# A tuned transformer kernel on one core: the seven-product scheme for gate and up of four feed-forward stages

## The chip, the core and the metric

The kernel runs on one core of a Trainium2 chip. The metric is the device time of one execution in microseconds (us), the median of several runs. The core's engines run side by side, each with its own queue that is worked off in order, and they wait for each other by semaphores: TensorE (PE in the rows; PEld is its loading of weights), VectorE (DVE), ScalarE (ACT), GpSimd (POOL) and SyncE (SP), which here issues the loads of weights.

## The reference, cut to what matters

Two transformer blocks follow each other on 512 tokens of width 1024. The first has two layers, each with a feed-forward part, a mixer and another feed-forward part; the second has 16 more tokens in front, and again a feed-forward part, a mixer and a feed-forward part. That makes six feed-forward stages with an inner width of 2816:

```python
def swiglu_ffn(x, w_gu, w_down):
    a, u = jnp.split(x @ w_gu, 2, axis=-1)
    return (jax.nn.silu(a) * u) @ w_down

def first_block(x, w_in, w_out, ...):
    for l in range(DEPTH):
        x = layer_norm(DEEPNORM_ALPHA * x + 0.5 * swiglu_ffn(x, ffn1_w_gu[l], ffn1_w_down[l]), ...)
        x = layer_norm(DEEPNORM_ALPHA * x + hybrid_mixer(x, ...), ...)
        x = layer_norm(DEEPNORM_ALPHA * x + 0.5 * swiglu_ffn(x, ffn2_w_gu[l], ffn2_w_down[l]), ...)
    return x
```

The change concerns the four feed-forward stages of the first block, and in them the products with `w_gu` (gate and up).

## The kernel before

**Layout.** Activations are kept with features on the partitions: `x` is 8 tiles (k) of 128 features by 512 tokens. A matmul multiplies a weight tile of 128x128 with 512 columns of one such tile. Every product is formed in three parts for precision: a number is split into a high part, rounded to the matmul's format, and a low part, the rest. The three are high weight by high x, low weight by high x, and high weight by low x. `pe_piece` (L387) does that: for each k three matmuls at L397, L400 and L403, all added up in one bank of PSUM.

**Weights.** They come in pieces of 128x1024 (8 tiles of 128x128, 512 KB). SP loads piece u into `w_raw[u % 4]` (`sp_load`), ACT casts it to `w_hi` (`act_split`, L340), and DVE subtracts to get `w_lo` (`dve_split`, L351). There are four slots of `w_hi`/`w_lo` in a ring; a cast waits until the piece that had its slot has been used by TensorE. A load waits for the low part of the piece that had its `w_raw`. In mixers GpSimd makes some of the low parts (L366).

**A feed-forward stage** (`ffn`, L480). There are 22 pairs of pieces: gate tile f and up tile f. TensorE does piece after piece (48 matmuls of 512 columns for a pair). ACT then makes silu of the gate product out of PSUM (L574), DVE multiplies it by the up product (L596), ACT casts the result to `h_hi` (L578), and DVE makes `h_lo` (L606). Then 8 tiles of the down product follow, each in three pieces, and the norm (`FfnNorm`, `MixNorm`). The order on each engine is written out by hand: the loops `ffn_pe`, `ffn_act` and `ffn_dve` run over steps s, one for each piece, with splits three pieces ahead. The first 3 or 5 pieces of three of these stages are done as a group, since x comes out of the norm tile by tile; the very first stage has no group.

**Elsewhere.** `Prepare` puts a small table of the second block (a product of 383 columns, some short operations, a store) into the first stage. The two feed-forward stages of the second block, the mixers and the norms go by the same lines and aren't touched, apart from slots.

## Time and profile before

| what | value |
|---|---|
| median of 3 runs | 3092.79 us (3091.29 to 3094.11) |
| span of the profiled execution | 3090.1 us |
| TensorE busy | 3043.6 us, 98% of the span |
| weight loads (PEld) busy | 2548.2 us, 82% |
| VectorE busy | 1421.9 us, 46% |
| ScalarE busy | 1158.2 us, 37% |
| GpSimd busy | 379.7 us, 12% |

The runs are about 2.7 us longer than the span that the profile covers, from the first to the last instruction of the program. The duration of a matmul in a row is that of one in a pipeline, so neighbours overlap: what it costs is read from the distance of the starts.

### The profile page before, as it was taken

What the parts mean: (1) busy time and instruction counts of PE and PEld (TensorE: products, weight loads), DVE (VectorE), ACT (ScalarE), POOL (GpSimd) and SP (SyncE); (2) the same over time, 40 slices, a digit from 0 to 9 for tenths busy, and PEclk for the clock granted to TensorE, in tenths of its full rate; (3) what the DMA queues carried; (4) which work ended last, traced back from release to release, by engine and by line L of the source; (5) the groups of instructions that cost most, each with busy time, mean ns of one, the idle gap of its engine ahead of it and who ended that gap; (6) DMA issues with size and microseconds to landing.
All of it is one profiled execution on the core that took longest, in us unless ns stands there. A gap on an engine that the chain in (4) does not pass through costs nothing.

```text
span 3090.1 us, 39392 instructions
## 1 busy us (share of the span) xinstructions
PE 3043.6 (98%) x16494; PEld 2548.2 (82%) x16494; DVE 1421.9 (46%) x2120; ACT 1158.2 (37%) x1868; POOL 379.7 (12%) x319
## 2 busy tenths in 40 slices
PE   9999999999999999999999999899999999999999
PEld 7888877888888888887788888899999767788888
DVE  4333465653335333356583333744423766554432
ACT  3322376442223322146553221522223456543221
POOL 0000143300001000014320000200002323200000
PEclk9999999999999999999999999999999999999999
DMA  4223331132332322332123223222233211122232
GB/s 161 96 94 89 93 103 62 55 110 96 94 93 66 117 95 92 94 118 67 55 76 103 95 90 95 75 96 89 86 89 102 80 38 35 41 95 93 93 93 77
DMA packets 76496, 269.62 MB, mean 87 GB/s; under 512 B 8720, under 2 KB 9008, under 8 KB 76064
## 3 DMA queue, kind: packets, MB, share of 16 engines
q1 hardware_dynamic: 74448, 260.08, 26.3%
q0 software_dynamic: 1872, 7.04, 0.7%
q8 instruction: 130, 2.13, 0.3%
q14 instruction: 46, 0.38, 0.0%
HBM read 264.97 MB, written 2.11 MB: 86 GB/s over the span
## 4 chain that ended last, share of the span: by engine, by line
PE 90%; DVE 7%; ACT 2%; issue 1%; DMA 0%; SPq 0%; POOL 0%; DVEq 0%; ACTq 0%
PE psum L397 25%; PE psum L400 25%; PE psum L403 25%; PE psum L461 3%; PE psum L473 2%; PE psum L416 1%; PE psum L420 1%; PE psum L418 1%; PE psum L696 1%; PE psum L2840 1%; DVE z_sum L853 1%; DVE x L865 1%; DVE x L858 1%; DVE b_rank L3115 0%; PE psum L1881 0%
## 5 line engine op out<-in xcount | busy, mean ns | idle before, releaser
L351 DVE TENSOR_TENSOR w_lo<-w_raw,w_hi 128x1024 fp32r<-128x1024 f32 (+1 forms) x444 | 554.7, 1251 | 1260.5 <-ACT w_hi L340 1260.4
L397 PE MATMUL psum<-x_hi,w_hi 128*128 128x512 f32 (+1 forms) x2800 | 964.0, 368 | 1.1 <-ACT neg_mean L2911 0.8
L400 PE MATMUL psum<-x_hi,w_lo 128*128 128x512 f32 (+1 forms) x2800 | 949.8, 363 | 0.9 <-DVE w_lo L351 0.9
L403 PE MATMUL psum<-x_lo,w_hi 128*128 128x512 f32 (+1 forms) x2800 | 945.2, 362 | 0.1
L340 ACT CAST w_hi<-w_raw 128x1024 fp32r<-128x1024 f32 (+1 forms) x490 | 503.7, 1029 | 1172.7 <-PE psum L403 1137.1
L397 PEld LDWEIGHTS psum<-x_hi,w_hi 128*128 128x128 f32 x2800 | 500.0, 188 | 109.0 <-issue 18.6
L400 PEld LDWEIGHTS psum<-x_hi,w_lo 128*128 128x128 f32 x2800 | 499.6, 188 | 88.0 <-issue 4.8
L403 PEld LDWEIGHTS psum<-x_lo,w_hi 128*128 128x128 f32 x2800 | 500.4, 189 | 84.7 <-DVE x_lo L3349 0.4
L397 PE MATMUL psum<-h_hi_ffn,w_hi 128*128 128x512 f32 (+1 forms) x792 | 296.9, 375 | 0.0
L400 PE MATMUL psum<-h_hi_ffn,w_lo 128*128 128x512 f32 (+1 forms) x792 | 292.2, 369 | 0.0
L403 PE MATMUL psum<-h_lo_ffn,w_hi 128*128 128x512 f32 (+1 forms) x792 | 290.7, 367 | 0.0
L397 PEld LDWEIGHTS psum<-h_hi_ffn,w_hi 128*128 128x128 f32 x792 | 149.0, 188 | 28.6 <-issue 1.0
L403 PEld LDWEIGHTS psum<-h_lo_ffn,w_hi 128*128 128x128 f32 x792 | 148.8, 188 | 28.2
L400 PEld LDWEIGHTS psum<-h_hi_ffn,w_lo 128*128 128x128 f32 x792 | 148.6, 188 | 27.2 <-issue 1.0
L366 POOL TENSOR_TENSOR w_lo<-w_raw,w_hi 128x512 fp32r<-128x512 f32 x92 | 119.7, 1324 | 248.6 <-ACT w_hi L340 248.5
L397 PE MATMUL psum<-h_hi_b_ffn,w_hi 128*128 128x264 f32 (+2 forms) x550 | 148.6, 316 | 0.0
L400 PE MATMUL psum<-h_hi_b_ffn,w_lo 128*128 128x264 f32 (+2 forms) x550 | 148.1, 315 | 0.0
L403 PE MATMUL psum<-h_lo_b_ffn,w_hi 128*128 128x264 f32 (+2 forms) x550 | 147.7, 314 | 0.0
L1031 POOL TENSOR_TENSOR z_sum<-x 128x512 f32<-128x512 f32 x4 | 5.2, 1299 | 1054.7 <-DVE x L1003 1054.7
L578 ACT CAST h_hi_ffn<-hid 128x512 fp32r<-128x512 f32 x88 | 54.6, 621 | 163.8 <-DVE hid L596 163.8
L403 PEld LDWEIGHTS psum<-h_lo_b_ffn,w_hi 128*128 128x128 f32 x550 | 93.2, 188 | 7.1
L397 PEld LDWEIGHTS psum<-h_hi_b_ffn,w_hi 128*128 128x128 f32 x550 | 93.1, 188 | 7.0
(386 smaller groups left out, 3388.3 us busy)
## 6 DMA issues: line engine op xcount, KB each, us to landing
w_raw<-in_ffn_gu SPq DMA_DIRECT2D x176, 512.0 KB, 3.3
w_raw<-in_ffn_down SPq DMA_DIRECT2D x64, 512.0 KB, 3.5
w_raw<-in_w_in SPq DMA_DIRECT2D x44, 512.0 KB, 3.3
w_raw<-in_b_gate SPq DMA_DIRECT2D x44, 512.0 KB, 3.3
w_raw<-in_b_up SPq DMA_DIRECT2D x44, 512.0 KB, 3.3
w_raw<-in_b_down SPq DMA_DIRECT2D x32, 512.0 KB, 3.5
w_raw<-in_ffn_down SPq DMA_DIRECT2D x32, 384.0 KB, 3.1
w_raw<-in_b_in SPq DMA_DIRECT2D x24, 512.0 KB, 3.3
```

Source lines behind the costliest of these rows:

```text
L340: nc.scalar.copy(w_hi[s][:, 0:n], w_raw[r][:, 0:n]).then_inc(*w_high.inc(u))
L351: nc.vector.tensor_tensor(w_lo[s][:, 0:n], w_raw[r][:, 0:n], w_hi[s][:, 0:n].bitcast(F32), ALU.subtract).then_inc(*w_low_dve.inc(u))
L366: nc.gpsimd.tensor_tensor(w_lo[s][:, c], w_raw[r][:, c], w_hi[s][:, c].bitcast(F32), ALU.subtract).then_inc(*w_low_pool.inc((u, half)))
L397: nc.tensor.matmul(out, w_h, hi[:, c], start=first and i == 0, stop=False)
L400: nc.tensor.matmul(out, w_l, hi[:, c], start=False, stop=False)
L403: done = nc.tensor.matmul(out, w_h, lo[:, c], start=False, stop=final and i == n - 1)
L416: nc.tensor.matmul(out, w_h, hi[:, c], start=j == 0, stop=False)
L418: nc.tensor.matmul(out, w_l, hi[:, c], start=False, stop=False)
L420: done = nc.tensor.matmul(out, w_h, lo[:, c], start=False, stop=j == KT // 2 - 1)
L461: nc.tensor.matmul(out, w_h, x_part[:, c], start=first, stop=False, skip_group_check=True)
L473: done = nc.tensor.matmul(out, w_l, x_hi[:, k, c], start=False, stop=k == KT - 1, skip_group_check=True)
L578: nc.scalar.copy(h_hi[:, f - 1, cols], hid[(f - 1) % 2][:, cols]).then_inc(*h_high.inc(f - 1))
```

## The change

In the stages `ffn1_0`, `ffn2_0`, `ffn1_1` and `ffn2_1` the pairs f = 0 to 3 stay as they were. Pairs 4 to 21 go through a new class `Combined`. It takes gate and up together as a 2 by 2 product of blocks: the two halves of the contraction (4 tiles of k each) and the two halves of the tokens (a and b, 256 columns each). With G1, G2 and U1, U2 for the two halves of a gate and an up piece, and X1a, X1b, X2a, X2b for the quarters of x, eight block products become seven:

| product | weights | x | bank |
|---|---|---|---|
| m1 | G1 | X1a | P |
| m2 | G2 | X2a | Q |
| m3 | s4 = s2 + G2 | X2b | R |
| m4 | U2 | t4 = -n2 - X2a | P |
| m5 | s1 = U1 + U2 | n1 = X1a - X1b | R |
| m6 | s2 = s1 + G1 | n2 = -n1 - X2b | P |
| m7 | s3 = U1 + G1 | t3 = X2b - X1b | P |

Gate a is m1 + m2; gate b is m1 + m6 + m5 + m3; up b is the negative of m1 + m6 + m7 + m5; up a is the negative of m1 + m6 + m7 + m4. Each product is 4 k by 3 parts, 12 matmuls of 256 columns.

What is new besides the products:

- x side, once a stage, in steps s = 1 to 5 of the direct part: `dve_turned`, `act_turned`, `dve_turned_low` make n1, n2, t3, t4 with high and low parts, 16 operations of DVE and 8 of ACT on 512 columns. t3 and t4 are put where `x` lies (`x_turned`); after the last m4 GpSimd rebuilds x as `x_hi + x_lo` (`pool`, 8 operations), and the norm waits for that (`rebuilt`).
- weight side, for each pair: DVE makes the sums s1, s2, s4 (into `sq_sum`, `square`) and s3 (into `w_raw` in place). The splits are of five blocks instead of two pieces: s1 and s3 (512 columns each, one slot), gate (1024), up's second half (512), and s2 with s4 as one ("later", 1024).
- results, for each pair: ACT copies three intermediate results out of PSUM (`act_copy`: r after m5, p1 after m1, p2 after m6). DVE joins gate a, gate b and up b, and makes h in two halves (`dve_first_half`, `dve_second_half`). silu now reads SBUF. The cast and the low part of h stay.
- `slot_plan` gives the four slots fixed roles in these pairs (sums, gate, up, later). `w_raw` of a gate piece is given back after s3, that of an up piece after the low part of its second half.
- the first down piece is done between m7 and m4 of the last pair (`fill`).
- `h_hi` and `h_lo` have 512 columns instead of 528, the tables of `Prepare` get their own places, `Prepare` moves to other steps, and GpSimd's scratch memory for DMAs is set to 4096.

```diff
+COMBINED = {"ffn1_0": 4, "ffn2_0": 4, "ffn1_1": 4, "ffn2_1": 4}
+HALF_K = KT // 2
+WIDTH = SEQ // 2
+            def pe_product(self, name, f):
...
+                for k in range(HALF_K):
...
+                    pe.wait_ge(*self.high.at((block, f)))
+                    nc.tensor.matmul(self.out(b), w_h, hi, start=opens and k == 0, stop=False,
+                                     skip_group_check=True)
+                    pe.wait_ge(*self.low.at((block, f)))
+                    nc.tensor.matmul(self.out(b), w_l, hi, start=False, stop=False,
+                                     skip_group_check=True)
+                    done = nc.tensor.matmul(self.out(b), w_h, lo, start=False,
+                                            stop=k == HALF_K - 1, skip_group_check=True)
+            def pe(self, fill):
...
+                for f in range(first, FT + 1):
+                    if f <= last:
+                        pe.wait_ge(*(self.joined.at(("gate_b", f - 2)) if f >= first + 2
+                                     else self.direct_left(self.r_bank(f))))
+                        self.pe_product("m5", f)
+                    if f > first:
+                        pe.wait_ge(*self.copied.at(("p2", f - 1)))
+                        self.pe_product("m7", f - 1)
+                    if f <= last:
...
+                        self.pe_product("m1", f)
+                        pe.wait_ge(*(self.joined.at(("gate_a", f - 1)) if f > first
+                                     else self.direct_left(self.q_bank)))
+                        self.pe_product("m2", f)
+                    else:
+                        fill()
+                    if f > first:
+                        pe.wait_ge(*self.joined.at(("up_b", f - 1)))
+                        self.pe_product("m4", f - 1)
+                    if f <= last:
+                        pe.wait_ge(*self.copied.at(("p1", f)))
+                        self.pe_product("m6", f)
+                        pe.wait_ge(*self.copied.at(("r", f)))
+                        self.pe_product("m3", f)
...
+            def act_high(self, name, f):
...
+                elif name == "later":
+                    act.wait_ge(*self.summed.at(("s4", f)))
...
+                if f > self.f0:
+                    act.wait_ge(*self.product_made.at((used_by, f - 1)))
...
+            def act_hidden(self, f):
+                act.wait_ge(*self.first_half.at(f))
+                act.wait_ge(*self.second_half.at(f))
+                nc.scalar.copy(self.h_hi[:, f, :], self.h[f % 2][:, TOK]).then_inc(
...
+            def pool(self):
+                pool.wait_ge(*self.product_made.at(("m4", FT - 1)))
...
-    nc = bacc.Bacc("TRN2", target_bir_lowering=False, num_devices=1)
+    nc = bacc.Bacc("TRN2", target_bir_lowering=False, num_devices=1,
+                   dynamic_dma_scratch_size=4096)
```

**The order on TensorE**, at the start of the first combined pair of the first stage. A row is one matmul with its columns; `t_hi` and `t_lo` are n1 and n2 of the x side. Before, in the middle of a piece:

```order
L397 MATMUL psum<-x_hi,w_hi0 128x512
L400 MATMUL psum<-x_hi,w_lo0 128x512
L403 MATMUL psum<-x_lo,w_hi0 128x512
L397 MATMUL psum<-x_hi,w_hi0 128x512
L400 MATMUL psum<-x_hi,w_lo0 128x512
```

After, where m5 ends and m1 begins:

```order
L677 MATMUL psum<-t_hi_ffn1_0,w_hi0 128x256
L680 MATMUL psum<-t_hi_ffn1_0,w_lo0 128x256
L682 MATMUL psum<-t_lo_ffn1_0,w_hi0 128x256
L677 MATMUL psum<-x_hi,w_hi1 128x256
L680 MATMUL psum<-x_hi,w_lo1 128x256
L682 MATMUL psum<-x_lo,w_hi1 128x256
```

A pair is now 84 matmuls of 256 columns in products of 12, where it was 48 of 512.

**The order on VectorE** in the middle of gate and up. Before, one pair and the start of the next:

```order
L596 TENSOR_TENSOR hid1<-hid1,psum 128x512
L351 TENSOR_TENSOR w_lo0<-w_raw0,w_hi0 128x1024
L606 TENSOR_TENSOR h_lo_ffn1_0<-hid1,h_hi_ffn1_0 128x512
L351 TENSOR_TENSOR w_lo1<-w_raw1,w_hi1 128x1024
L596 TENSOR_TENSOR hid0<-hid0,psum 128x512
```

After, twelve of the fifteen operations of a step: gate b, later low, s3, up b, s3 low, s1, s2, s4, gate a, s1 low, gate low, first half. The second half (L875, 256 columns), up low (L811, 512) and h low (L881, 512) follow.

```order
L849 TENSOR_TENSOR hid0<-psum,z_sum 128x256
L811 TENSOR_TENSOR w_lo3<-square,w_hi3 128x1024
L832 TENSOR_TENSOR w_raw3<-w_raw3,w_raw2 128x512
L857 SCALAR_TENSOR_TENSOR up_b_ffn1_0<-psum,neg_mean 128x256
L811 TENSOR_TENSOR w_lo0<-w_raw3,w_hi0 128x512
L832 TENSOR_TENSOR sq_sum<-w_raw1 128x512
L832 TENSOR_TENSOR square<-sq_sum,w_raw0 128x512
L832 TENSOR_TENSOR square<-square,w_raw0 128x512
L844 TENSOR_TENSOR hid1<-psum,z_sum 128x256
L811 TENSOR_TENSOR w_lo0<-sq_sum,w_hi0 128x512
L811 TENSOR_TENSOR w_lo1<-w_raw0,w_hi1 128x1024
L866 SCALAR_TENSOR_TENSOR hid0<-psum,hid0 128x256
```

A pair is four operations before and fifteen after.

**The order on ScalarE** at the same place. Before:

```order
L574 ACTIVATE hid1<-psum 128x512
L340 CAST w_hi3<-w_raw3 128x1024
L578 CAST h_hi_ffn1_0<-hid1 128x512
L340 CAST w_hi0<-w_raw0 128x1024
L574 ACTIVATE hid0<-psum 128x512
```

After, one whole step: up high, h high, copy p2, later high, silu, copy r, s3 high, copy p1, s1 high, gate high.

```order
L749 CAST w_hi2<-w_raw1 128x512
L772 CAST h_hi_ffn1_0<-hid1 128x512
L766 COPY z_sum<-psum 128x256
L749 CAST w_hi3<-square 128x1024
L788 ACTIVATE hid0<-hid0 128x512
L766 COPY neg_mean<-psum 128x256
L749 CAST w_hi0<-w_raw3 128x512
L766 COPY z_sum<-psum 128x256
L749 CAST w_hi0<-sq_sum 128x512
L749 CAST w_hi1<-w_raw0 128x1024
```

A pair is four operations before and ten after; the later cast now stands behind the h cast and a copy.

## Rows read from the trace of the kernel before

**Rows 1.** The page: engines, clock in 40 slices, chain that ended last, loads.

```profile
PE 3043.6 (98%) x16494; PEld 2548.2 (82%) x16494; DVE 1421.9 (46%) x2120; ACT 1158.2 (37%) x1868; POOL 379.7 (12%) x319
...
PEclk9999999999999999999999999999999999999999
...
PE 90%; DVE 7%; ACT 2%; issue 1%; DMA 0%; SPq 0%; POOL 0%; DVEq 0%; ACTq 0%
...
w_raw<-in_ffn_gu SPq DMA_DIRECT2D x176, 512.0 KB, 3.3
```

**Rows 2.** Timeline, VectorE, first stage: start us, duration us, operation, [idle before].

```profile
31.99 1.23 DVE L351 TENSOR_TENSOR w_lo<-w_raw,w_hi 128x1024 fp32r<-128x1024 f32 x1 [3.73 <-ACT w_hi L340]
...
43.11 1.23 DVE L351 TENSOR_TENSOR w_lo<-w_raw,w_hi 128x1024 fp32r<-128x1024 f32 x1 [3.73 <-ACT w_hi L340]
```

**Rows 3.** Timeline, TensorE, last down tile of the first stage, 45 matmuls apart.

```profile
373.80 0.28 PE L403 MATMUL psum<-h_lo_ffn,w_hi 128*128 128x256 f32 x1
...
379.09 0.28 PE L403 MATMUL psum<-h_lo_ffn,w_hi 128*128 128x256 f32 x1
```

**Rows 4.** Timeline, TensorE, output product in runs of 12; a run begins at 603.75.

```profile
603.64 0.28 PE L420 MATMUL psum<-x_lo,w_hi 128*128 128x256 f32 x1
603.75 0.28 PE L416 MATMUL psum<-x_hi,w_hi 128*128 128x256 f32 x1
603.87 0.28 PE L418 MATMUL psum<-x_hi,w_lo 128*128 128x256 f32 x1
```

**Rows 5.** Groups by shape, 130 to 250 us: count, busy us, mean ns, idle.

```profile
L397 PEld LDWEIGHTS psum<-x_hi,w_hi 128*128 128x128 f32 x173 | 32.5, 188 | 7.8
...
L351 DVE TENSOR_TENSOR w_lo<-w_raw,w_hi 128x1024 fp32r<-128x1024 f32 x21 | 25.7, 1225 | 78.4 <-ACT w_hi L340 78.4
L340 ACT CAST w_hi<-w_raw 128x1024 fp32r<-128x1024 f32 x21 | 22.1, 1052 | 64.1 <-PE psum L403 64.1
...
L606 DVE TENSOR_TENSOR h_lo_ffn<-hid,h_hi_ffn 128x512 fp32r<-128x512 f32 x10 | 6.8, 685 | 0.0
L578 ACT CAST h_hi_ffn<-hid 128x512 fp32r<-128x512 f32 x11 | 6.8, 621 | 20.8 <-DVE hid L596 20.8
```

**Rows 6.** Groups by shape, whole span: other shapes of VectorE and ScalarE.

```profile
L858 DVE SCALAR_TENSOR_TENSOR x<-psum,x 128x256 f32<-128x256 f32 x96 | 36.9, 419 | 0.2
...
L1022 DVE TENSOR_TENSOR x<-x,neg_mean 128x512 f32<-128x512 f32 x24 | 14.8, 688 | 0.0
```

**Rows 7.** The same view, ScalarE.

```profile
L568 ACT ACTIVATE hid<-hid 128x512 f32<-128x512 f32 x22 | 13.9, 633 | 52.7 <-DVE hid L616 52.7
...
L2014 ACT CAST y_hi<-psum 128x256 fp32r<-128x256 f32 x16 | 5.9, 368 | 11.3 <-PE psum L1881 11.3
```

**Rows 8.** Timeline around 105 us: hand-overs and overlaps.

```profile
104.65 1.05 ACT L340 CAST w_hi<-w_raw 128x1024 fp32r<-128x1024 f32 x1 [1.73 <-PE psum L403]
...
105.60 0.59 ACT L574 ACTIVATE hid<-psum 128x512 f32<-128x512 f32 x1
105.73 1.22 DVE L351 TENSOR_TENSOR w_lo<-w_raw,w_hi 128x1024 fp32r<-128x1024 f32 x1 [3.46 <-ACT w_hi L340]
...
106.88 0.68 DVE L606 TENSOR_TENSOR h_lo_ffn<-hid,h_hi_ffn 128x512 fp32r<-128x512 f32 x1
```

**Rows 9.** Timeline, VectorE: an operation that needs the one before it.

```profile
2000.10 0.70 DVE L596 TENSOR_TENSOR hid<-hid,psum 128x528 f32<-128x528 f32 x1
2000.83 0.71 DVE L601 TENSOR_TENSOR hid<-hid,z_sum 128x528 f32<-128x528 f32 x1
```

**Rows 10.** Timeline around 2708 us: last matmul of a product, and its reader.

```profile
2707.78 0.28 PE L420 MATMUL psum<-x_lo,w_hi 128*128 128x256 f32 x1
...
2708.10 0.42 DVE L2338 TENSOR_TENSOR x<-x,psum 128x256 f32<-128x256 f32 x1 [1.00 <-PE psum L420]
```

**Rows 11.** The chain of waits at the program's start: start us, us, what.

```profile
5.20 6.52 DMA w_raw<-in_ffn_gu
```

**Rows 12.** Timeline, GpSimd, start of the second block's mixer.

```profile
2369.55 4.23 POOL L3223 DMA_DIRECT2D b_q_lat<-bias_rows  x8
...
2381.62 3.96 POOL L366 TENSOR_TENSOR w_lo<-w_raw,w_hi 128x512 fp32r<-128x512 f32 x2 [6.26 <-ACT w_hi L340]
```

More of the change, by code:

```diff
@@ L205, in widened, with combined_pieces @@
     return [n for n in first if n.startswith("mix_") or n in ("ffn2_0", "ffn2_1", "ffn1_1")]
+def combined_pieces(first):
+    return {first[name] + i: name for name, f0 in COMBINED.items()
+            for i in range(2 * f0, 2 * FT)}
 def slot_plan(plan, first):
@@ L218, in slot_plan @@
             own[u] = (SPLIT_SLOTS + i, first[name] - (OUT_PAIRS + 1 if from_mixer else 2))
-    slot, before, ring = [], [], []
+    combined = combined_pieces(first)
+    slot, before, roles = {}, {}, {}
+    ring = [(i, None) for i in range(SPLIT_SLOTS)]
     for u in range(len(plan)):
         if u in own:
-            slot.append(own[u][0])
-            before.append(own[u][1])
-        else:
-            slot.append(len(ring) % SPLIT_SLOTS)
-            before.append(ring[-SPLIT_SLOTS] if len(ring) >= SPLIT_SLOTS else None)
-            ring.append(u)
-    return slot, before
+            slot[u], before[u] = own[u]
+        elif u not in combined:
+            slot[u], before[u] = ring.pop(0)
+            ring.append((slot[u], u))
+        elif combined[u] not in roles:
+            name = combined[u]
+            roles[name] = dict(zip(("sums", "gate", "up", "later"), ring))
+            at, last = {role: i for role, (i, _) in roles[name].items()}, FT - 1
+            ring = [(at["gate"], (name, "m2", last)), (at["later"], (name, "m3", last)),
+                    (at["sums"], (name, "m7", last)), (at["up"], (name, "m4", last))]
+    return slot, before, roles
 def pool_pieces(plan, first):
@@ L273, in build @@
         sq_sum = sb("sq_sum", [P, LEN])
-        square = [sb(f"square{i}", [P, LEN]) for i in range(2)]
+        squares = sb("square", [P, 2, LEN])
+        square = [squares[:, i, :] for i in range(2)]
         ident = sb("ident", [P, P])
@@ L317, in build @@
         out_done = signal("out_done", out_keys)
-        w_used = signal("w_used", [u for u in everything if u not in out_first + out_second])
+        w_used = signal("w_used", [u for u in everything if u not in out_first + out_second
+                                   and u not in combined])
         def used(u):
+            if u in half_used:
+                return half_used[u]
             if u in out_first:
@@ L513, in held @@
             def held(i):
-                before = [j for j in range(i) if bank(j) == bank(i)]
+                before = [j for j in range(i) if bank(j) == bank(i)
+                          and not n_direct <= j < n_up]
+                if i >= n_up and f0 < FT and (i - n_up) < 4:
+                    return [half.bank_left(bank(i))]
                 if before:
@@ L580, in ffn_act, with dve_hidden @@
+                    if 2 <= s and s % 2 == 0:
+                        act_hidden(f - 1)
+                if half:
+                    half.act(lambda: act_hidden(f0 - 1), u_down,
+                             prepare.act_stored if prepare else None)
+                for s in range(n_up, n_up + 3 * KT - 2):
+                    act_split(u0 + s + AHEAD)
+                    if s == n_up and not half:
+                        act_hidden(FT - 1)
                     if s > n_up:
                         leave.act_after(*divmod(s - n_up, 3))
+            def dve_hidden(f):
+                dve.wait_ge(*silu.at(f))
+                dve.wait_ge(*w_used.at(u0 + 2 * f + 1))
+                h = view(hid[f % 2][:, cols])
+                made = nc.vector.tensor_tensor(h, h, product(bank(2 * f + 1)), ALU.mult)
+                if entry.late:
+                    made.then_inc(*dve_own.inc())
+                    dve.wait_ge(*dve_own.done())
+                    h = hid[f % 2][:, cols]
+                    made = nc.vector.tensor_tensor(h, h, z_sum[:, cols], ALU.mult)
+                made.then_inc(*gated.inc(f))
```

494 lines of the change are left out of this document (432 added, 62 removed).

## The prediction, made before the changed kernel ran

> **What bounds the kernel now.** I read the page's busy line and its chain first [rows 1]: TensorE is busy for 98% of the span, the chain that ended last runs over it for 90%, and its clock is full throughout. In gate and up the next question is its pace. VectorE's w_lo operations follow TensorE piece by piece, and one starts every 5.56 us ((43.11 - 31.99) / 2) with 3.73 us of idle time before it [rows 2]. So a pair of pieces takes 11.12 us, which is 48 matmuls at 0.2317 us, back to back. ScalarE waits for TensorE there and VectorE for ScalarE [rows 5]: both are slack. An edit that saves matmul columns saves time one for one, until another engine takes over.
>
> **TensorE's part.** A matmul of 256 columns isn't half of one of 512. In the last down tile 45 of them, each with its own weight load, take 379.09 - 373.80 = 5.29 us, 0.1176 us each [rows 3]; in the output product, whose runs of 12 are just the shape of the new products, it is 0.11 to 0.12 us, also where a run begins and its semaphores are waited for [rows 4]. I take 0.118. A pair is then 84 x 0.118 = 9.91 us. The saving is 1.21 us a pair, and there are 4 x 18 = 72 combined pairs: 87.1 us if TensorE never waits.
>
> A rule of the Trainium skill speaks against this: page "TensorE: Matmul & The Clock Gate", section "LDWEIGHTS (loading the stationary operand)", gives a load as its columns by 1.2 GHz, 107 ns here, and the same page says that pace comes from load and matmul together; if they added up, 107 + 107 = 214 ns x 84 would be an estimated 18.0 us a pair. By that rule the trace disagrees, since rows 3 hold both in 118 ns.
>
> **VectorE's part.** Durations: 1024 columns 1.225, 512 columns 0.685 (low part) and 0.688 (sum) [rows 5, 6], 256 columns with PSUM 0.42 [rows 6]. The second half of h, 256 columns from SBUF alone, has no row here; it lies between nothing and the 0.42 of the PSUM form, and I take 0.42. When its data is ready, an operation starts 0.07 to 0.08 us before the one ahead ends (106.88 against 105.73 + 1.22) [rows 8]; when it needs the result of the one ahead, 0.03 after it [rows 9]. So in a full queue they cost 1.14, 0.60 and 0.34. A pair has two of 1024, eight of 512 and five of 256: 2.28 + 4.80 + 1.70 = 8.8 us, and 0.24 more because s2 and s4 need the sum before. That is 9.0 us of 9.91, where it was 3.7 of 11.12 (11.12 - 2 x 3.73). ScalarE: 1.05 and 0.62 for casts [rows 5], 0.63 for silu, 0.37 for a copy out of PSUM [rows 7], with overlaps of 0.10 (105.60 against 104.65 + 1.05) [rows 8]; ten operations are about 5.3 us. Neither is over TensorE's pace by its sum.
>
> **The loop between them.** The orders tie the two together once a step, so I walk that loop with these durations and 0.03 us for a hand-over [rows 8]. From the second half of h on VectorE: ScalarE's h cast 0.65, copy p2 0.27, later cast 0.95; VectorE's later low 1.26 (with the hand-over), s3 0.60; ScalarE's s3 cast 0.65; VectorE's s3 low 0.72, s1 0.60, s2 0.72, s4 0.72, gate a 0.34, s1 low 0.60, gate low 1.14, first half 0.34, second half 0.34. The sum is 9.90 us. TensorE needs 9.91. **This tie is the centre of the prediction**: 1% on the loop is 0.1 us a pair, 7 us in all, and nothing in the trace runs these engines so densely.
>
> Does TensorE enter the loop? A product's result can be read 0.32 us after the start of its last matmul [rows 10], so 12 matmuls later counted from the product's start it is 0.2 behind the next product's start. Laying the step on TensorE's clock (m5 at 0, m7 1.4, m1 2.8, m2 4.2, m4 5.7, m6 7.1, m3 8.5), later low ends at about 3.4 and m6 needs it at 7.1; gate low ends at 9.4 and m1 needs it at 12.7; copy p2 ends at 1.2 and m7 needs it at 1.4. Only that last one is near, with 0.2 us. I take a pace of 9.95 us: TensorE's, with a little of the loop. The pairs then save 72 x (11.12 - 9.95) = 84.2 us.
>
> **First step of a stage.** Before the first m5 VectorE and ScalarE have time (5.56 us pieces), and the x side fits: 16 x 0.6 = 9.6 us on VectorE in the idle time that rows 2 show (3.7 us a piece, over five pieces). In the first combined step, though, h of the last direct pair is made on VectorE behind gate low of pair 5, which waits for the gate cast, which waits for m2. With m5 at 0, m2 is read at 4.4, s1 of pair 5 isn't low before 7.5, and m5 of pair 5 starts 0.45 late. Gate low ends at 8.6, h at 9.2, its cast at 9.9, copy p2 at 10.15, and m7 starts 1.25 us late. Four stages: 4 x 1.7 = 6.8 us lost. After that the engines stand as in the steady step.
>
> **End of a stage.** The first down piece (24 matmuls of 512, 5.6 us) stands ahead of the last m4, and the second behind it; h of the last pair is ready 2.5 us after m4. Nothing waits. GpSimd's rebuilding of x is 8 operations of some 1.3 us, and the first is due when the first down tile is finished, 9.7 us later: hidden. Table places, `Prepare`'s steps: the same operations elsewhere, nothing. The silu table is loaded once more in the first stage, a microsecond at most, hidden in part.
>
> **GpSimd's DMA scratch.** No row shows what a smaller one does. Lower bound nothing; upper bound that each of the eight loads at 2369.55 waits for the one ahead, 8 x 3.3 us (the time that a load of weights takes to land [rows 1]) instead of 4.23, 22 us later, of which 6.26 us of idle time cover some [rows 12]: 16 us. I take nothing, because the loads are few and small.
>
> **The sum.** 3090.1 - 84.2 + 6.8 = 3012.7 us of span. The median of the runs was 2.7 above the span: 3015.4, rounded to 3015.
>
> **Rivals.**
>
> - *The loop of VectorE and ScalarE sets the pace.* For it: the tie, fifteen short operations with up to three waits each, and PSUM and SBUF read by both at once. Against it: rows 8 show the overlap intact with two semaphores to wait for. At 1.5% to 5% more the pace is 10.05 to 10.4 us, and TensorE waits about 0.15 to 0.5 us in each step, mostly ahead of m7. That gives 3023 to 3048 us.
> - *No overlap on VectorE.* If its operations don't overlap, the seven of the loop that I priced with an overlap (s3, s1, gate a, s1 low, gate low, the two halves) lose 0.08 each: the loop is 9.90 + 0.56 = 10.46 us, say 10.5 with what I took for the pace above it, and 72 x 0.55 = 40 us more: 3055. Rows 8 speak against it. The Trainium skill, page "VectorE: DVE Perf Modes", section "The DRAIN you can't avoid", says that the next operation doesn't start until the pipe is empty, which would be this case; by that rule the trace disagrees, with a start 0.07 us before the end ahead.
> - *Slower: the load of the up piece.* Its `w_raw` comes free only with up low, the second to last operation of a step (at 10.7 of the step), and s1 of the pair after next needs the new piece at 15.2, so 4.5 us are left. The loop is load + 5.5 us. At the median of 3.3 us [rows 1] it is 8.8 us and hidden; with the 6.52 us that a load took at the start, with many in flight [rows 11], it is 12.0 us: 72 x 0.9 = 65 us slower than before, 3165 with the first steps. It decides from a load of 5.6 us. The 1.05 MB of a pair now come in 9.91 us instead of 11.12, a rate 12% higher, which isn't the crowding of the start; so it is unlikely.
> - *The change doesn't do what it says.* TensorE's order shows products of 12 with 256 columns, so this is excluded, but single waits that I haven't seen, such as GpSimd's ring (up to 16 us) or a clash of GpSimd's rebuilding with VectorE, give 3020 to 3035.
>
> **How the numbers follow.** Forecast (3006 to 3022) 0.50; loop sets the pace (3022 to 3048) 0.33; no overlap (3050 to 3065) 0.05; waits not seen (3020 to 3035) 0.06; slower by loads or weight loads 0.03; under 3006 0.03, since 3092.8 - 87.1 is the floor. The range 3006 to 3046 holds the forecast, the unseen waits and most of the loop's case: some 0.85. About 0.2%, 6 us, can be told from no change; all but the slow case are beyond it. Faster 0.95, same 0.02, slower 0.03.
>
> **What the profile after would show.** Right: the starts of later low on VectorE 9.9 to 10.0 us apart; 256-column matmuls 0.118 us apart; VectorE busy for nine tenths of these stretches, TensorE's idle time a microsecond or two at each stage's first step. The loop: the same starts 10.05 us or more apart, and TensorE's wait ahead of m7 ended by ScalarE's copy p2, or ahead of m5. No overlap: VectorE's starts a full duration apart. Loads: VectorE waiting at s1 for a DMA. The prediction is wrong if the short operations last longer beside each other than in the rows used here, or if a wait costs the engine time even when it is met.

## The result, and the profile after

| | before | changed |
|---|---|---|
| median of the runs | 3092.07 us (3091.29 to 3094.11, 4 runs) | 3023.18 us (3021.21 to 3025.22, 4 runs) |
| span of the profiled execution | 3090.1 us | 3021.2 us |
| that execution's own time | | 3022.54 us |

The changed kernel takes 0.9777 of the time before (95% interval 0.9763 to 0.9791): 68.9 us less. The forecast was 3015, with a range of 3006 to 3046. The time is 8 us over the forecast. It lies in the range, but just outside the forecast's own case (to 3022) and at the lower edge of the rival "the loop of VectorE and ScalarE sets the pace" (3023 to 3048), and that rival is what the profile shows.

The page of the changed kernel, to be held against [rows 1]: engines, the clock in 40 slices, the chain that ended last, the load of a piece (its median time to landing, in us), and one group of TensorE's matmuls (busy us, mean ns, idle us before them).

```profile
PE 2968.8 (98%) x19086; PEld 2619.6 (87%) x19086; DVE 1884.6 (62%) x2976; ACT 1348.9 (45%) x2332; POOL 439.9 (15%) x351
...
PEclk9999999999999999999999999999999999999999
...
PE 85%; DVE 9%; ACT 3%; issue 2%; DMA 0%; SPq 0%; POOL 0%; DVEq 0%; ACTq 0%
...
L677 PE MATMUL psum<-x_turned,w_hi 128*128 128x256 f32 x576 | 169.2, 294 | 4.5 <-ACT z_sum L766 4.3
...
w_raw<-in_ffn_gu SPq DMA_DIRECT2D x176, 512.0 KB, 3.6
```

The granted clock is the same as before, 0.996 in the mean of both traces. The sign that something has changed hands is the chain: TensorE's share fell from 90% to 85%, and VectorE's and ScalarE's rose from 7% and 2% to 9% and 3%. TensorE's busy share of 98% says nothing of it. In 160 us of steady steps of the second stage its idle time is nought, while VectorE is busy for 91% (busy time by stretch: PE, PEld, DVE, ACT, POOL, with the number of instructions):

```profile
660.00:820.00 160.00, 160.00 (x1343) 159.16 (x1342) 145.79 (x237) 89.54 (x159) 0.00 (x0) 1.00 0.35 105
```

**The pace of a pair.** The starts of later low on VectorE count the steps. In the second stage (an operation, count, shortest, median and longest duration in ns, first and last start):

```profile
L811 DVE TENSOR_TENSOR w_lo<-square,w_hi x16: 1224/1225/1226, 653.7 to 804.2; 128x1024 fp32r<-128x1024 f32 x16
```

That is (804.2 - 653.7) / 15 = 10.03 us a pair. In all four stages a steady step takes 10.02 to 10.04 us, with two longer ones (10.23 and 10.32) in the first stage.

**Where TensorE waits though it has no idle time.** Its timeline and that of its weight loads at the place where m7 begins, and ScalarE's copy p2 (start us, duration us, operation):

```profile
702.78 0.28 PE L682 MATMUL psum<-t_lo_ffn,w_hi 128*128 128x256 f32 x1
702.93 0.39 PE L677 MATMUL psum<-x_turned,w_hi 128*128 128x256 f32 x1
703.16 0.28 PE L680 MATMUL psum<-x_turned,w_lo 128*128 128x256 f32 x1
```

```profile
702.67 0.19 PEld L682 LDWEIGHTS psum<-t_lo_ffn,w_hi 128*128 128x128 f32 x1
702.93 0.19 PEld L677 LDWEIGHTS psum<-x_turned,w_hi 128*128 128x128 f32 x1
```

```profile
702.51 0.37 ACT L766 COPY z_sum<-psum 128x256 f32<-128x256 f32 x1
```

Copy p2 ends at 702.88. The weight load of m7's first matmul, due one matmul earlier, stands at 702.93, and the matmul of the same start lasts 0.39 us instead of 0.28. The next one follows after 0.23 us instead of 0.12. So 0.11 us is lost in every step, and the record shows it as a longer matmul, not as idle time. In the group above it is the mean of 294 ns. The deadline of copy p2 is one matmul sooner than the start of m7, because the weights are loaded ahead.

**The loop, walked in the changed kernel.** VectorE and ScalarE over one step of the second stage, to be read with the terms of the prediction:

```profile
702.78 1.05 ACT L749 CAST w_hi<-square 128x1024 fp32r<-128x1024 f32 x1
...
705.73 0.62 ACT L749 CAST w_hi<-w_raw 128x512 fp32r<-128x512 f32 x1 [1.10 <-DVE w_raw L832]
...
712.02 0.62 ACT L772 CAST h_hi_ffn<-hid 128x512 fp32r<-128x512 f32 x1 [2.22 <-DVE hid L875]
```

```profile
703.86 1.23 DVE L811 TENSOR_TENSOR w_lo<-square,w_hi 128x1024 fp32r<-128x1024 f32 x1 [0.19 <-ACT w_hi L749]
705.00 0.69 DVE L832 TENSOR_TENSOR w_raw<-w_raw 128x512 f32<-128x512 f32 x1
...
706.38 0.69 DVE L811 TENSOR_TENSOR w_lo<-w_raw,w_hi 128x512 fp32r<-128x512 f32 x1 [0.35 <-ACT w_hi L749]
706.99 0.69 DVE L832 TENSOR_TENSOR sq_sum<-w_raw 128x512 f32<-128x512 f32 x1
707.78 0.69 DVE L832 TENSOR_TENSOR square<-sq_sum,w_raw 128x512 f32<-128x512 f32 x1
708.50 0.69 DVE L832 TENSOR_TENSOR square<-square,w_raw 128x512 f32<-128x512 f32 x1
709.11 0.42 DVE L844 TENSOR_TENSOR hid<-psum,z_sum 128x256 f32<-128x256 f32 x1
709.45 0.68 DVE L811 TENSOR_TENSOR w_lo<-sq_sum,w_hi 128x512 fp32r<-128x512 f32 x1
710.05 1.22 DVE L811 TENSOR_TENSOR w_lo<-w_raw,w_hi 128x1024 fp32r<-128x1024 f32 x1
711.18 0.42 DVE L866 SCALAR_TENSOR_TENSOR hid<-psum,hid 128x256 f32<-128x256 f32 x1
711.52 0.42 DVE L875 TENSOR_TENSOR hid<-up_b_ffn,hid 128x256 f32<-128x256 f32 x1
```

Taken from end to end, thirteen of the fifteen terms stand within 0.01 us of what was written down: for instance later low 703.83 to 705.09 = 1.26, s3 low 706.35 to 707.07 = 0.72, gate low 710.13 to 711.27 = 1.14. Two don't. The cast of h starts 0.08 us after the end of the second half (711.94, 712.02) and takes 0.70 from there, not 0.65. The sum s2 starts 0.10 us after the end of s1 (707.68, 707.78), while s4, which also needs the result of the operation ahead, starts 0.03 after s2 (708.47, 708.50): 0.79, not 0.72. With these two the walk comes to 10.02, and the starts show 10.03.

What the two have in common: in the code each waits for two semaphores, and the one that comes last stands second. In the trace the second wait is an instruction of its own (at 144.148 to 144.165 us on ScalarE, 0.03 us after the second half's end at 144.117, and the cast of h only at 144.205). Operations with one wait, or whose last semaphore is the first of two, like the s3 cast, start 0.03 to 0.04 us after it. The first two experiments test whether this is where the time is.

**First steps.** At each stage's second m5 and at the m7 behind it (second stage):

```profile
650.14 0.39 PE L680 MATMUL psum<-t_hi_ffn,w_lo 128*128 128x256 f32 x1 [0.23 <-DVE w_lo L811]
...
652.79 0.38 PE L677 MATMUL psum<-x_turned,w_hi 128*128 128x256 f32 x1 [1.08 <-ACT z_sum L766]
```

By the distances of the starts m5 loses 0.49 us and m7 1.35, 1.84 us together.

### The profile page after: what moved, and what is told of

It reads as the page before. It is cut to its first block, busy times and chain, and to the rows that moved or that the text cites. A ratio compares the mean times of both kernels' runs of the same rounds, so it can differ in the third digit from the quotient of the medians.

```text
span 3021.2 us, 46552 instructions
## 1 busy us (share of the span) xinstructions
PE 2968.8 (98%) x19086; PEld 2619.6 (87%) x19086; DVE 1884.6 (62%) x2976; ACT 1348.9 (45%) x2332; POOL 439.9 (15%) x351
## 4 chain that ended last, share of the span: by engine, by line
PE 85%; DVE 9%; ACT 3%; issue 2%; DMA 0%; SPq 0%; POOL 0%; DVEq 0%; ACTq 0%
PE psum L424 17%; PE psum L427 17%; PE psum L430 17%; PE psum L677 7%; PE psum L682 7%; PE psum L680 6%; PE psum L488 3%; PE psum L500 2%; DVE w_lo L811 1%; PE psum L443 1%; PE psum L447 1%; PE psum L445 1%; PE psum L1216 1%; ACT w_hi L749 1%; PE psum L3364 1%
## 5 line engine op out<-in xcount | busy, mean ns | idle before, releaser
L424 PE MATMUL psum<-x_hi,w_hi 128*128 128x512 f32 (+1 forms) x1648 | 511.8, 352 | 1.4 <-ACT neg_mean L3435 0.7
L427 PE MATMUL psum<-x_hi,w_lo 128*128 128x512 f32 (+1 forms) x1648 | 494.0, 341 | 0.9 <-DVE w_lo L377 0.9
L430 PE MATMUL psum<-x_lo,w_hi 128*128 128x512 f32 (+1 forms) x1648 | 492.3, 340 | 0.1
L424 PEld LDWEIGHTS psum<-x_hi,w_hi 128*128 128x128 f32 x1648 | 283.6, 189 | 57.3 <-issue 18.4
L427 PEld LDWEIGHTS psum<-x_hi,w_lo 128*128 128x128 f32 x1648 | 283.4, 189 | 37.6 <-issue 4.8
L430 PEld LDWEIGHTS psum<-x_lo,w_hi 128*128 128x128 f32 x1648 | 283.5, 189 | 36.0 <-DVE x_lo L3873 0.6
L677 PE MATMUL psum<-x_hi,w_hi 128*128 128x256 f32 x864 | 242.7, 281 | 0.0
L682 PE MATMUL psum<-x_lo,w_hi 128*128 128x256 f32 x864 | 242.1, 280 | 0.0
L680 PE MATMUL psum<-x_hi,w_lo 128*128 128x256 f32 x864 | 241.9, 280 | 0.0
L811 DVE TENSOR_TENSOR w_lo<-w_raw,w_hi 128x512 fp32r<-128x512 f32 (+1 forms) x216 | 186.7, 865 | 27.3 <-ACT w_hi L749 27.3
```

The source lines that it names most:

```text
L424: nc.tensor.matmul(out, w_h, hi[:, c], start=first and i == 0, stop=False)
L427: nc.tensor.matmul(out, w_l, hi[:, c], start=False, stop=False)
L430: done = nc.tensor.matmul(out, w_h, lo[:, c], start=False, stop=final and i == n - 1)
L677: nc.tensor.matmul(self.out(b), w_h, hi, start=opens and k == 0, stop=False, skip_group_check=True)
L680: nc.tensor.matmul(self.out(b), w_l, hi, start=False, stop=False, skip_group_check=True)
L682: done = nc.tensor.matmul(self.out(b), w_h, lo, start=False, stop=k == HALF_K - 1, skip_group_check=True)
```

## The experiments

**Theory A**: the loop of VectorE and ScalarE sets the pace, at 10.03 us, and TensorE only touches it at copy p2. **Theory B**: the loop closes through TensorE, over copy p2 and m7. **Theory C**: TensorE's matmuls are slower here. A fourth, by VectorE's busy time, stands where it expects something else.

The experiments have short names. E1_swap_s2 and e2_swap_both exchange waits, e3_p2_early moves copy p2, e4 gives TensorE less to do, e5_all_fixes takes all the improvements together, e6 is e5 with less for TensorE, e7 and e8 add an operation to VectorE, e9 gives h low to GpSimd, e10 combines one stage only, and e11 changes the DMA scratch alone. E2 and e3 ran four times and e5 five times; the others ran once, and a single span is uncertain by some 2 us either way. So the argument goes by the paces, which hardly vary. The kernel before took 3091.4 to 3091.6 us beside the experiments and 3092.1 beside the changed kernel, so the differences between medians are good to about 1 us.

The pace in these experiments is read as above, from the starts of later low in the second stage.

### One pair of waits, then both

```diff
-                    dve.wait_ge(*loaded[u % RAW_SLOTS].at(u))
                     dve.wait_ge(*self.summed.at(("s1", f)))
+                    dve.wait_ge(*loaded[u % RAW_SLOTS].at(u))
```

> The changed kernel with one edit: VectorE's sum s2 waits for sum s1 first and for its load second, instead of the other way round. In the trace of the changed kernel the second of two waits stands as an instruction of its own, and s2 starts 0.10 us after the end of s1, where s4, with one wait, starts 0.03 after s2. Theory A (the loop of VectorE and ScalarE, walked through s1, s2 and s4, sets the pace at 10.03 us): s2 starts 0.03 to 0.04 us after s1, the loop is 0.06 to 0.07 us shorter, the starts of later low are 9.96 to 9.97 us apart, and the span falls by about 4 us, to 3017. Theory B (only the chain second half, h cast, copy p2, m7 is late, and it closes through TensorE): s2 is not in it, the pace stays 10.03 and the span within 1 us of 3021. Theory C (the matmuls themselves are slower here): the same as B.

```profile
L811 DVE TENSOR_TENSOR w_lo<-square,w_hi x16: 1224/1225/1226, 654.0 to 803.3; 128x1024 fp32r<-128x1024 f32 x16
```

The pace is (803.3 - 654.0) / 15 = 9.95 us, the span 3015.7. An exchange of two waits on VectorE, far from copy p2 and m7, took 0.08 us from every step. That speaks for theory A and against B and C. The fall of the span, 5.5 us, is a little more than 72 x 0.07.

The same edit, and in ScalarE's cast of h:

```diff
-                act.wait_ge(*self.first_half.at(f))
                 act.wait_ge(*self.second_half.at(f))
+                act.wait_ge(*self.first_half.at(f))
```

> The changed kernel with both pairs of waits the other way round: s2 as in e1_swap_s2, and ScalarE's h cast, which waits for the second half first and for the first half second; in the changed kernel it starts 0.10 us after the second half ends. Theory A: both starts come 0.06 to 0.07 us sooner, the loop is 10.03 - 0.13 = 9.90 us, TensorE's 84 x 0.118 = 9.91 takes over, and the pace is 9.91 to 9.93. The long first matmul of m7 (0.39 us instead of 0.28) goes in the steady steps. Span 3021.2 - 72 x 0.11 = 3013.5, give or take 1.5. Theory B: 9.96 and 3016. Theory C: 10.03 and 3021.

The median is 3015.17 us (3014.07 to 3019.19), 0.9751 of the time before (0.9734 to 0.9767), 8.0 us under the changed kernel. The profiled execution was the longest of the four, with a span of 3017.9 and a granted clock of 0.995 in the mean. The other three, at 0.996 to 0.997, had 3012.8, 3013.4 and 3014.4, where 3013.5 was expected. Its pace, VectorE around s2, and the matmuls with `x_turned` (m4 and m7) over 160 us (mean ns):

```profile
L811 DVE TENSOR_TENSOR w_lo<-square,w_hi x17: 1224/1226/1227, 653.2 to 811.7; 128x1024 fp32r<-128x1024 f32 x17
```

```profile
705.85 0.69 DVE L832 TENSOR_TENSOR sq_sum<-w_raw 128x512 f32<-128x512 f32 x1
706.57 0.69 DVE L832 TENSOR_TENSOR square<-sq_sum,w_raw 128x512 f32<-128x512 f32 x1
```

```profile
L677 PE MATMUL psum<-x_turned,w_hi 128*128 128x256 f32 x129 | 36.3, 281 | 0.0
```

s2 now starts 0.03 us after s1 (706.54, 706.57), as s4 does. The pace is (811.7 - 653.2) / 16 = 9.91 us. That is the loop's own: TensorE alone takes 9.93, as the next experiment shows, so VectorE only gains a lead of 0.02 us a step. The long first matmul of m7 is gone: 281 ns in the mean instead of 294. So the two terms that the walk had too low are the whole of the difference between 9.90 and 10.03, and what removes them is the order of two waits.

### Copy p2 earlier

```diff
+                    if first <= f <= last:
+                        self.act_copy("p2", f)
                     if f == first:
                         hidden()
                     elif f > first:
                         self.act_hidden(f - 1)
-                    if first <= f <= last:
-                        self.act_copy("p2", f)
```

> The changed kernel with ScalarE's copy p2 moved ahead of the cast of h in each step; nothing else. The product that it reads, m6, is ready some 1.4 us before the second half of h is. Theory A: 0.27 us leave the loop (9.76), TensorE sets the pace at 9.91, and in each stage's first step m7 no longer waits behind the last direct h (1.24 us). Span 3021.2 - 7.7 - 4 x 1.3 = 3008, give or take 1.5. Theory B gives the same here, since p2 is what TensorE waits for. Theory C (TensorE's matmuls are slower, no wait): pace 10.03, only the first steps' 5 us go, 3016.

The median is 3011.20 us (3010.71 to 3012.17), 0.9739 of the time before (0.9725 to 0.9754), the span 3009.4: within the 1.5 us allowed. The pace shows two stretches, 690 to 758 us and 778 to 807 us:

```profile
L811 DVE TENSOR_TENSOR w_lo<-square,w_hi x8: 1225/1226/1227, 689.8 to 758.1; 128x1024 fp32r<-128x1024 f32 x8
```

```profile
L811 DVE TENSOR_TENSOR w_lo<-square,w_hi x4: 1225/1226/1226, 777.7 to 807.5; 128x1024 fp32r<-128x1024 f32 x4
```

First VectorE makes a step in (758.1 - 689.8) / 7 = 9.76 us, just the loop without copy p2's 0.27, while TensorE goes at its own pace. VectorE's lead grows until it needs something from TensorE, and from there a step takes (807.5 - 777.7) / 3 = 9.93 us. That is TensorE's pace, 84 x 0.1182 us, slightly above my 9.91.

### Less work for TensorE

```diff
-                    nc.tensor.matmul(self.out(b), w_l, hi, start=False, stop=False,
-                                     skip_group_check=True)
+                    if k < HALF_K - 1:
+                        nc.tensor.matmul(self.out(b), w_l, hi, start=False, stop=False,
+                                         skip_group_check=True)
```

> The changed kernel with 77 matmuls a pair instead of 84: each of the seven products leaves out the last of its four products with the weights' low part. TensorE then needs 77 x 0.118 = 9.09 us a pair. Theory A: the pace stays 10.03 us, because the loop of VectorE and ScalarE has it; TensorE waits about 0.95 us a step, and the span falls by at most 2 us in the first and last steps. Theory B (the loop closes through TensorE's products): the pace falls by some of the 0.82 us, to 9.3 to 9.9. Theory C (TensorE sets the pace): 9.2, and the span falls by 59 us.

```profile
L812 DVE TENSOR_TENSOR w_lo<-square,w_hi x16: 1224/1226/1226, 655.0 to 805.5; 128x1024 fp32r<-128x1024 f32 x16
```

```profile
704.20 0.39 PE L677 MATMUL psum<-x_turned,w_hi 128*128 128x256 f32 x1 [0.66 <-ACT z_sum L767]
```

TensorE has 8% less to do in these stages, and the pace is (805.5 - 655.0) / 15 = 10.03 us as before, the span 3020.8. TensorE's wait for copy p2 is now idle time, 0.66 us a step, besides the longer matmul. This excludes theories B and C.

### All of it together

The two exchanges of waits, copy p2 early, and s1 low ahead of gate a:

```diff
+                    if f < last:
+                        self.dve_low("s1", f + 1)
                     if first <= f <= last:
                         self.dve_join("gate_a", f)
                     if f < last:
-                        self.dve_low("s1", f + 1)
                         self.dve_low("gate", f + 1)
```

> The changed kernel with copy p2 ahead of the h cast, both pairs of waits the other way round, and VectorE's s1 low ahead of gate a instead of behind it. The last is aimed at the 0.49 us (0.53 in e3_p2_early) that m5 of a stage's second combined pair waits for s1 low, which stands behind gate a and with it behind m2. Theory A: the loop is 10.03 - 0.13 - 0.27 = 9.63 us, TensorE's 9.91 to 9.93 sets the pace as in e3_p2_early, and only the 4 x 0.53 us of the first steps come on top: span 3009.4 - 2.1 = 3007.3, give or take 1. If s1 low isn't what m5 of that pair waited for, or the next thing behind it is as late, 3009.4.

The median of five is 3010.31 us (3009.00 to 3012.68), 0.9736 of the time before (0.9723 to 0.9750): the fastest kernel here, 12.9 us under the changed one. The span is 3009.2, only 0.2 below e3_p2_early. The wait of m5 is gone, but the next thing is nearly as late (TensorE, second stage): m4 of the first pair waits for up b, 0.31 us, worked out from the starts as above.

```profile
652.99 0.28 PE L682 MATMUL psum<-x_lo,w_hi 128*128 128x256 f32 x1
653.32 0.38 PE L677 MATMUL psum<-x_turned,w_hi 128*128 128x256 f32 x1
653.54 0.28 PE L680 MATMUL psum<-x_turned,w_lo 128*128 128x256 f32 x1
```

That is 0.2 of 0.5 us gained a stage, less than two executions differ by.

This kernel also answers for the rival "the load of the up piece". Its loop is short enough for a slow load to show:

```profile
670.36 1.23 DVE L811 TENSOR_TENSOR w_lo<-square,w_hi 128x1024 fp32r<-128x1024 f32 x1
...
674.15 0.69 DVE L832 TENSOR_TENSOR sq_sum<-w_raw 128x512 f32<-128x512 f32 x1 [0.58 <-DMA w_raw<-in_ffn_gu]
...
680.67 1.23 DVE L811 TENSOR_TENSOR w_lo<-square,w_hi 128x1024 fp32r<-128x1024 f32 x1
```

```profile
L406 SPq DMA_DIRECT2D w_raw<-in_ffn_gu x1: 328/328/328, 669.4 to 669.4; - x1
...
DMA to landing us min/median/max: 4.8/4.8/4.8
```

The load took 4.8 us, VectorE waited 0.58 us for it at s1, and the step took 680.67 - 670.36 = 10.31 us: the prediction's "load + 5.5". TensorE lost nothing by it, since VectorE had a lead. In the changed kernel the same load was issued at 692.50 and s1 started at 696.96, so it has 4.46 us (4.5 in the prediction) against a median of 3.6.

### The loop laid bare

The kernel of e5 with the edit of e4.

> e5_all_fixes with 77 matmuls a pair instead of 84 (each product leaves out the last of its four products with the weights' low part), so that TensorE needs 9.09 us a pair and the loop of VectorE and ScalarE is laid bare. Theory A: later low starts every 9.63 us, give or take 0.05, and TensorE waits in every step. Theory B (TensorE's products are a part of the loop): 9.3 or less. Theory C: 9.2 at most, TensorE's own.

```profile
L812 DVE TENSOR_TENSOR w_lo<-square,w_hi x11: 1224/1226/1227, 703.1 to 799.4; 128x1024 fp32r<-128x1024 f32 x11
```

(799.4 - 703.1) / 10 = 9.63 us, to the hundredth what the walk gives. One earlier step of this stage took 9.97. The time is 2987.28 us, but this kernel leaves out products, so it is no candidate. With TensorE out of the way nothing but the fifteen terms, less 0.27 and 0.13, sets the pace.

### The same operation in the loop and beside it

```diff
+                    if first < f <= last:
+                        one = self.t_hi[:, 0, 0, 0:P].bitcast(F32)
+                        nc.vector.tensor_tensor(self.spare[:], one, one, ALU.mult)
```

with `spare` a tile of its own of 128 columns; ahead of gate a:

> The changed kernel with one more operation of VectorE in each combined step but the first, 128 columns from SBUF, placed between s4 and gate a. By the prices of 256 and 512 columns in a full queue, 0.34 and 0.60 us, it costs about 0.21 us there. Theory A: it stands in the loop, the pace is 10.03 + 0.21 = 10.24 us, and the span rises by 67 x 0.21 = 14 us to 3035. Theory B (the chain second half, h cast, copy p2, m7 through TensorE) and C: 10.03 us and 3021.

and ahead of h low:

> The same additional operation as in e7_extra_in, placed between up low and h low, where VectorE waits for ScalarE anyway (h low starts 0.22 us later than the full queue would let it, and later low 0.27 us). VectorE's busy time is that of e7_extra_in. Theory A: this stretch is beside the loop, which goes over ScalarE here, so the pace stays 10.03 to 10.05 us and the span 3021 to 3023. A theory by VectorE's busy time expects the same as for e7_extra_in, 3035.

The paces of the one and of the other:

```profile
L812 DVE TENSOR_TENSOR w_lo<-square,w_hi x14: 1224/1224/1226, 669.0 to 802.0; 128x1024 fp32r<-128x1024 f32 x14
```

```profile
L812 DVE TENSOR_TENSOR w_lo<-square,w_hi x16: 1224/1225/1226, 653.5 to 803.9; 128x1024 fp32r<-128x1024 f32 x16
```

(802.0 - 669.0) / 13 = 10.23 us and a span of 3036.8 in the one place; (803.9 - 653.5) / 15 = 10.03 us and 3018.7 in the other. The work is the same, 0.28 us of VectorE in each step, and so a busy share can't tell the two apart. It costs 0.20 us a step where the loop runs over VectorE. Where the loop runs over ScalarE it costs nothing, since VectorE has 0.22 us to spare there, about what the operation takes.

### h low by GpSimd

```diff
-                dve.wait_ge(*self.h_high.at(f))
-                nc.vector.tensor_tensor(
+                pool.wait_ge(*self.h_high.at(f))
+                nc.gpsimd.tensor_tensor(
```

with its calls moved from VectorE's order to GpSimd's.

> The changed kernel with h's low part of the 72 combined pairs made by GpSimd instead of VectorE: 0.60 us a step leave VectorE's queue. Theory A: h low is not in the loop, which goes over ScalarE's casts at that point, so nothing is gained: the pace is 10.03 us at best. GpSimd and VectorE beside each other are both slower in the trace of the changed kernel (an addition of 512 columns on GpSimd 1.3 us alone and 1.92 us beside VectorE), so gate b, later low or s3 may last longer: up to 0.6 us a step, which gives 10.03 to 10.6 us and a span of 3021 to 3062; I expect about 10.3 and 3040. A theory by VectorE's busy time expects 10.03 - 0.60, so TensorE's 9.93 us, and 3012.

```profile
L811 DVE TENSOR_TENSOR w_lo<-square,w_hi x16: 1224/1225/1226, 655.2 to 805.6; 128x1024 fp32r<-128x1024 f32 x16
```

```profile
704.13 1.30 POOL L881 TENSOR_TENSOR h_lo_ffn<-hid,h_hi_ffn 128x512 fp32r<-128x512 f32 x1 [8.73 <-ACT h_hi_ffn L772]
```

The pace is 10.03 us again and the span 3023.0, though VectorE was relieved of one operation in fifteen. No gain, as theory A says; the theory by busy time is wrong by 11 us. My guess of some 0.3 us for the two engines beside each other was wrong as well: GpSimd took 1.30 us, and VectorE's later low at most 1.226. Here GpSimd's operation lies beside gate b and VectorE's wait for the later cast.

### What the rest of the change costs

```diff
-COMBINED = {"ffn1_0": 4, "ffn2_0": 4, "ffn1_1": 4, "ffn2_1": 4}
+COMBINED = {"ffn1_0": 4}
```

> The changed kernel with only the first feed-forward stage combined and the other three as before; the small DMA scratch, the places of tiles and all else stay. If the gain lies in the combined pairs alone and the rest costs nothing: the first stage saves what it saves in the changed kernel, 16.96 us, and the span is 3090.1 - 17.0 = 3073.1, give or take 1.5. If something else of the change costs time in the rest of the program, it is more than 3075.

The span is 3076.0, 14.1 us less than before, where 17.0 were expected. The first stage itself gave 16.7 us, counted at the end of its down product. The remaining 2.6 us have two sources, which the traces show.

The first is the down products. The last one of the program, before and in the changed kernel (first and last matmul):

```profile
2965.08 0.40 PE L397 MATMUL psum<-h_hi_b_ffn,w_hi 128*128 128x512 f32 x1
...
3087.62 0.28 PE L403 MATMUL psum<-h_lo_b_ffn,w_hi 128*128 128x256 f32 x1
```

```profile
2895.66 0.39 PE L424 MATMUL psum<-h_hi_b_ffn,w_hi 128*128 128x512 f32 x1
...
3018.73 0.28 PE L430 MATMUL psum<-h_lo_b_ffn,w_hi 128*128 128x256 f32 x1
```

The same 594 matmuls take 123.07 us instead of 122.54, though this stage isn't combined. In e10 they take 123.07 too, and those of each of the three stages that e10 leaves direct take 126.39 instead of 125.98: 3 x 0.41 + 0.53 = 1.8 us in all. With the small scratch alone (e11, below) they last what they lasted before. The down product over 528 columns, whose `h_hi` and `h_lo` kept their width, takes 130.13 us in all these kernels. So the cost comes with the new width or the new places of `h_hi` and `h_lo`; which of the two, no run separates.

The second is TensorE's clock, which falls to the lower of its two levels (1.2 GHz instead of 2.4) for short stretches, in other places from one execution to the next. One of them lies in e10's mixer after the first stage (busy times by engine as above; the third number from the right is the granted clock in the mean):

```profile
429.00:439.00 10.00, 9.39 (x54) 6.96 (x54) 6.97 (x10) 4.63 (x14) 4.11 (x2) 0.83 0.09 17
```

In the 10 us ahead of it TensorE was busy for 8.7. A matmul at 429.90 still starts 16.73 us sooner than the same one before (446.63), one at 435.48 only 15.17 us (450.65), and there the kernel before has a granted clock of 1.00. This takes 1.6 us. Further on e10 gains and loses such amounts again, so the balance of 0.8 us that the down products leave is no more than the clock moves.

```diff
-    nc = bacc.Bacc("TRN2", target_bir_lowering=False, num_devices=1)
+    nc = bacc.Bacc("TRN2", target_bir_lowering=False, num_devices=1,
+                   dynamic_dma_scratch_size=4096)
```

> The kernel before with the DMA scratch of 4096 bytes and nothing else. My bounds were nothing and 16 us. With nothing: span 3090.1, give or take 1.5, and the eight small loads ahead of the second block's mixer last what they lasted before, 4.23 us together. With the bound: these loads one after the other, 26 us, and a span of 3106.

```profile
2369.24 4.25 POOL L3223 DMA_DIRECT2D b_q_lat<-bias_rows  x8
```

The span is 3089.8 us, and the eight loads of [rows 12] last 4.25 us instead of 4.23. In this run the small scratch costs nothing that shows; the upper bound of 16 us is refuted.

## Why the prediction was right, and where it was off

**TensorE's part: right.** 256-column matmuls in runs of 12, each with its own weights, follow each other every 0.118 us, as [rows 3, 4] had it. Its pace without waits is 9.93 us where I took 9.91, 1.4 us over 72 pairs. The rule of the Trainium skill that I set against it (page "TensorE: Matmul & The Clock Gate", section "LDWEIGHTS (loading the stationary operand)") gives the load as its columns by 1.2 GHz, 107 ns here. Taken as load and matmul adding up it would have given an estimated 18.0 us a pair; the trace of the changed kernel disagrees with that, with both in 0.118 us. The adding up was my reading: the same page of the Trainium skill, section "Back-to-back issue gap", calls the two pipelined, and with this the trace agrees.

**The loop: the right mechanism, two of its terms too small.** The prediction had the loop at 9.90 against TensorE's 9.91 and called the tie the centre. It took 0.03 us for a hand-over everywhere, by [rows 8, 9]. The cast of h cost 0.05 more and s2 0.07 more, because in both the semaphore that comes last is the second of two waits. The loop was thus 10.03, over TensorE's 9.93. So what came is the first rival, given 0.33, and not the forecast's own case, given 0.50, where TensorE sets the pace; the range held because it covered both. The pace that I took, 9.95, was 0.08 too short: 72 x 0.08 = 5.8 us of the 8.5 by which the span of 3021.2 exceeds the sum's 3012.7. The step that failed is "fifteen short operations with up to three waits each", set aside with [rows 8]. Those rows show overlap with waits that were met long before, and what counts in the loop is the wait that comes last. E1 and e2 show that it was this, and e6, at the 9.63 that the walk gives, that no other term is missing.

**The place of TensorE's wait: right, its deadline off by a matmul.** "Only that last one is near, with 0.2 us" named copy p2 and m7. The weight load ahead of m7 does the waiting, so only 0.1 was left.

**First step of a stage: right.** 0.45 and 1.25 us were predicted, and 0.49 and 1.35 came, for the reasons given: 4 x 1.84 = 7.4 us instead of 6.8. E3 removed the second wait, and e5 exchanged the first for another.

**The remaining 2 us of the span: a term put at nothing.** "Table places, `Prepare`'s steps: the same operations elsewhere, nothing" left out, with the narrower `h_hi` and `h_lo`, that the down products would run slower. They take 0.5 us more in the last one and about 0.4 in each of the four of the combined stages, 2.1 us together (the section on e10 has the rows). Two long steps of the first stage (10.23 and 10.32) add 0.5, and the first step of each stage, 9.90 from one later low to the next, takes 0.5 off. Against it the profiled run was only 1.3 us above its own span; the 2.7 had set a median against the span of one execution. The silu table is not loaded once more either: the first stage has two such loads in both traces, of 1.28 us each.

**Loads: right.** 4.46 us to spare against my 4.5, and e5 shows the loop of load + 5.5 where a load takes longer. **DMA scratch: right**, nothing (e11). **GpSimd's rebuilding of x: hidden, but mispriced.** It takes 1.92 us an operation, not 1.3 (all 32 operations: busy us, mean ns), and VectorE beside it is slower too. In the changed kernel at the end of the first stage, the second half's 256 columns take 1.28 us instead of 0.42, and four low parts 8.51:

```profile
L932 POOL TENSOR_TENSOR x<-x_hi,x_lo 128x512 f32<-128x512 f32 x32 | 60.4, 1920 | 917.4 <-PE psum L682 917.4
```

```profile
243.30 1.28 DVE L875 TENSOR_TENSOR hid<-up_b_ffn,hid 128x256 f32<-128x256 f32 x1
...
246.21 8.51 DVE L377 TENSOR_TENSOR w_lo<-w_raw,w_hi 128x768 fp32r<-128x768 f32 x4
```

TensorE has two down pieces queued there and loses nothing.

**The rival "no overlap": didn't happen.** In the walked step first half starts 0.09 us before gate low ends (711.18 against 711.27). The section "The DRAIN you can't avoid" of the Trainium skill's page "VectorE: DVE Perf Modes" first says that the next operation doesn't start until the pipe is empty; taken alone, the trace disagrees with that here too. The same section adds that a next operation that isn't held starts earlier, which I had left out, and this the trace bears out.

## What to carry to other kernels

When the sums of two or three engines come within a few per cent, walk the loop that ties them, from end to end, and find for each of its operations which wait comes last and as what it is issued: two exchanges of waits were worth 8 us here, and a copy moved ahead in its engine's order 12 us, while an operation less for the engine that is busy for 91% was worth nothing. Then ask where the tied engine touches the bound one, and take what it waits for off the loop. An engine's idle time doesn't show a wait shorter than the pipeline: compare the mean duration of the first matmul of a group, or the distances of starts.

## What the runs showed of the hardware that I had not expected

- A second wait ahead of an operation is an instruction of its own. When it is met last, the operation starts 0.08 to 0.10 us after the end of what it waited for; when the wait met last stands first in the code, 0.03 to 0.04 us. When both were met long before, the overlap of 0.08 us with the operation ahead is intact.
- The wait for a matmul holds its weight load, which is due one matmul earlier (0.12 us at 256 columns). A wait of 0.11 us appeared as a matmul of 0.39 us instead of 0.28, with no idle time.
- GpSimd and VectorE slowed each other down strongly in one place and not in another: an operation of 512 columns on GpSimd took 1.92 us beside a queue of VectorE operations from SBUF (of which 768 columns took about 2.1 us each, and 256 columns 1.28 instead of 0.42), and 1.30 us beside an operation that reads PSUM and a wait (e9). What makes the difference was not tested.
- The same matmuls on the same data took 0.3 to 0.4% longer in the down products (123.07 us instead of 122.54 for 594 of them) once `h_hi` and `h_lo` had 512 columns instead of 528 and lay elsewhere.
